# Sparse attention of 64 items: four buffers, memory keys and half of the memory values inside its loop, items looked ahead in another order

## The reference, cut to what matters

```python
y_conv = conformer_conv(conv_a, conv_b, w_dw, b_dw, ln_g, ln_b)   # depthwise conv of 31 taps, layer norm, SiLU
out = g[..., 0:1] * o_cmp + g[..., 1:2] * o_slc + g[..., 2:3] * o_win   # compressed, selected, window attention
h = h + jnp.concatenate([y_conv, y_nsa], axis=-1) @ w_out
h = h + memory_attention(rmsnorm(h, g1), rmsnorm(mem, g2), w_mem_q, w_mem_k, w_mem_v, w_mem_o)
h = h + peer(rmsnorm(h, g3), ...)   # 16 experts of 16384 for each of 8 heads and every token, gathered by rows
```

## Time and profile before

| | us |
|---|---|
| median of 3 runs | 2980.44 (2977.33 to 2980.55) |
| profiled execution | 2980.34, span 2978.5 |
| mean granted clock of TensorE | 0.907 |
| TensorE, VectorE, ScalarE, GpSimd busy in the span | 2604.3, 1440.5, 643.2, 596.9 |
| sparse attention loop (first score matmul to last value matmul) | about 1044 to 1286 |
| first matmul of the output product | 1325.84 |

### The profile page before, as it was taken

One profiled execution on the slowest core, in us unless ns is written; L12 is line 12 of the kernel. 1 busy time (PEld: TensorE's weight loads), 2 busy tenths in 40 slices (PEclk: granted clock), 3 DMA queues, 4 the chain that ended last, 5 costly groups with the idle time before them and its releaser, 6 DMA issues.

```text
span 2978.5 us, 22380 instructions
## 1 busy us (share of the span) xinstructions
PE 2604.3 (87%) x7486; PEld 1261.2 (42%) x7486; DVE 1440.5 (48%) x3647; ACT 643.2 (22%) x1514; POOL 596.9 (20%) x554
## 2 busy tenths in 40 slices
PE   6999999989979989999999899877778778778787
PEld 2456544435534545554454344333333333333232
DVE  0003113035342855322013666777777777777774
ACT  2000012116320132221122222222222122222221
POOL 0000000000000000000000243444444444344442
PEclk8999899999989975589999999999998998898988
DMA  8101042200111200012212899999999999999996
GB/s 350 56 29 57 28 184 85 85 0 1 43 49 60 85 15 0 1 57 85 85 43 95 322 380 378 420 421 421 421 422 421 421 421 420 419 418 416 417 412 264
DMA packets 83154, 648.49 MB, mean 218 GB/s; under 512 B 9329, under 2 KB 9617, under 8 KB 10978
## 3 DMA queue, kind: packets, MB, share of 16 engines
q0 software_dynamic: 75696, 551.95, 45.0%
q1 hardware_dynamic: 7346, 95.12, 8.4%
HBM read 644.93 MB, written 2.10 MB: 217 GB/s over the span
## 4 chain that ended last, share of the span: by engine, by line
PE 61%; DMA 23%; DVE 9%; ACT 2%; issue 2%; POOL 1%; ACTq 0%; DVEq 0%; POOLq 0%; SPq 0%; PEldq 0%
PE psum L506 23%; DMA arena<-in_peer_uv,newton 22%; PE psum L1057 12%; PE psum L1026 3%; PE psum L580 3%; PE psum L871 2%; PE psum L888 2%; DVE arena L1871 2%; PE psum L879 1%; PE psum L562 1%; PE psum L539 1%; PE psum L675 1%; PE psum L725 1%; PE psum L943 1%; ACT arena L1093 1%
## 5 line engine op out<-in xcount | busy, mean ns | idle before, releaser
L1057 PE MATMUL psum<-arena 128*128 128x512 f32 x2048 | 1006.9, 648 | 249.1 <-ACT arena L1371 248.7
L1057 PEld LDWEIGHTS psum<-arena 128*128 128x128 f32 x2048 | 415.3, 208 | 834.9 <-issue 834.8
L1871 DVE CUSTOM_DVE_ANT_0 arena<-arena 128x1024 f32<-128x1024 f32 x512 | 619.5, 1223 | 304.2 <-DMA arena<-in_peer_uv,newton 301.1
L2004 POOL DMA_INDIRECT arena<-in_peer_uv,newton x512 | 566.3, 1106 | 859.2 <-PE psum L1057 711.7
L506 PE MATMUL psum<-arena 128*128 128x512 f32 (+2 forms) x1824 | 698.2, 543 | 22.2 <-DVE arena L1543 8.0
L506 PEld LDWEIGHTS psum<-arena 128*128 128x128 f32 (+1 forms) x1824 | 346.3, 191 | 369.3 <-issue 347.9
L1093 ACT ACTIVATE arena<-psum 128x512 f32<-128x512 f32 (+8 forms) x335 | 177.5, 542 | 968.0 <-PE psum L506 398.1
L1371 ACT ACTIVATE arena<-ident,newton 128x128 f32<-128x128 f32 x512 | 166.5, 391 | 247.2 <-DVE newton L1880 240.2
L1362 ACT ACTIVATE arena<-arena 128x4 f32<-128x4 f32 (+1 forms) x148 | 30.2, 204 | 658.6 <-DVE arena L1871 658.5
L1026 PE MATMUL psum<-arena 128*128 128x512 f32 x256 | 119.3, 603 | 4.8 <-DVE arena L1543 4.5
L1599 DVE TENSOR_REDUCE small<-psum 128x1 f32<-128x768 f32 (+1 forms) x48 | 37.4, 780 | 123.4 <-PE psum L959 85.0
(11 more groups left out here) (257 smaller groups left out, 2022.4 us busy)
## 6 DMA issues: line engine op xcount, KB each, us to landing
arena<-in_weights SPq DMA_DIRECT2D x44, 2048.0 KB, 8.5
arena<-in_peer_uv,newton POOLq DMA_INDIRECT x512, 18.5
arena<-in_xin POOLq DMA_DIRECT2D x1, 3072.0 KB, 16.8
arena<-in_dft_l POOLq DMA_DIRECT2D x1, 2048.0 KB, 14.1
arena<-in_cmp_w POOLq DMA_DIRECT2D x1, 2048.0 KB, 7.5
out<-arena SPq DMA_DIRECT2D x4, 512.0 KB, 10.0
arena<-in_pool_band POOLq DMA_DIRECT2D x1, 1280.0 KB, 5.8
arena<-in_fnet_w POOLq DMA_DIRECT2D x1, 1024.0 KB, 20.8
```

The source lines that it names most:

```text
L1057: ins = mm(bank(j_y[t][q]), DIAG[i % 4], ROW[ROW_PLACE[i]][:, D + 512 * q:D + 512 * q + 512], start=(r == 0), stop=(r == 127))
L1871: v.tensor_tensor_reduce(out=u, in0=u, in1=HNT[:, i // 128, :], scale=1.0, scalar=0.0, op0=ALU.mult, op1=ALU.add, accum_out=DOTS[:, i:i + ...
L2004: g.indirect_dma_start(out=ROW[ROW_PLACE[i]][:, :], out_offset=None, in_=a["peer_uv"], in_offset=bass.IndirectOffsetOnAxis(ap=IDX[:, n, e: ...
```

## The change

`SM`, `P2` and `PT2` get four buffers each; other areas move to make room. The scores take banks 0 and 1 in turn instead of three, and bank 2 serves the memory keys, the sum of the conv output and the first half of the memory values, one job after the other.

TensorE's order for i becomes transposes of i, values of i-2, a memory step, scores of i+4 last; VectorE's is normalise i, masked maximum of i+3; ScalarE's is exponential of i+1, copy of i-1. A memory step is two 128x256 matmuls of the memory keys in items 10 to 33 and 38 to 45, and one 128x512 matmul of the memory values' first half in items 46 to 61. The memory norm moves to items 1 to 13, the conv taps to one in each of items 0 to 31, and the conv norm into items 34 to 49: sum at 34, centring at 35, squares at 37, second sum at 41, variance at 42, root at 43, inverse at 44, scaling at 46, SiLU at 49. The weights of the memory values are cut into two blocks: the first comes ahead of the output product's blocks, the second stays behind them. Behind the loop only the second half of the values is left.

```diff
-          ("mem_k", 2), ("out2", 2), ("mem_v", 2), ("mem_q", 2), ("mem_o", 2), ("peer_q", 4)]
+          ("mem_k", 2), ("mem_v_lo", 1), ("out2", 2), ("mem_v_hi", 1), ("mem_q", 2), ("mem_o", 2), ("peer_q", 4)]
...
-        SM = area(80, 2, L)
+        SM = area(88, 4, L)
...
-        P2 = area(72, 2, L)
-        PT2 = area(76, 2, L)
+        P2 = area(72, 4, L)
+        PT2 = area(80, 4, L)
...
-        SQ2 = area(72, 4, L)
+        SQ2 = area(144, 4, L)
...
-        MV = area(120, 2, D)
-        MQ = area(128, KC, L)
+        MV = area(136, 2, D)
+        MQ = area(96, KC, L)
...
-            if hh == 1:
+            if hh == 0:
                 j_rms_mem = [J.take(5)]
+            if hh == 5:
+                j_ln_cv_var = J.take(5)
             for m in range(8):
-                j_s2[8 * hh + m] = J.take((8 * hh + m) % 3)
+                j_s2[8 * hh + m] = J.take((8 * hh + m) % 2)
                 j_pt2[8 * hh + m] = J.take(3 + (8 * hh + m) % 2)
+        j_mk = [J.take(2) for _ in range(6)]
+        j_ln_cv = [[J.take(2)], [j_ln_cv_var]]
+        j_mk += [J.take(2) for _ in range(2)]
+        j_mv = [J.take(2) for _ in range(2)]
         J.align()
-        j_ln_cv = [J.turn(1)]
-        j_mk = J.turn(4)
-        j_ln_cv.append(J.turn(1))
-        j_mk += J.turn(4)
         j_rms_mq = J.turn(1)
         j_out2 = J.turn(8, [j_rms_mq[0][0]])
-        j_mv = J.turn(4)
+        j_mv += J.turn(2)
...
+            def memory_keys(c, first, last):
+                w = weights("mem_k", c // 4)
+                j = j_mk[c]
+                for k in range(first, last):
+                    if k == 0:
+                        claim(pe, j)
+                    pe.wait_ge(S["mem_ready"], k + 1)
+                    ins = mm(bank(j, LC), w[:, c % 4, k, :], MEMT[:, k, :], start=(k == 0), stop=(k == KC - 1))
+                if last == KC:
+                    done(ins, j)
+                    if c % 4 == 3:
+                        release_block(j)
+            def memory_values(b, t, first, last):
+                w = weights(("mem_v_lo", "mem_v_hi")[b], 0)
+                j = j_mv[2 * b + t]
...
+            def memory_step(i):
+                if 10 <= i < 34:
+                    n = i - 10
+                    memory_keys(n // 4, 2 * (n % 4), 2 * (n % 4) + 2)
+                elif 38 <= i < 46:
+                    n = i - 14
+                    memory_keys(n // 4, 2 * (n % 4), 2 * (n % 4) + 2)
+                elif 46 <= i < 62:
+                    n = i - 46
+                    memory_values(0, n // 8, n % 8, n % 8 + 1)
             cmp_scores(0)
-            for i in range(3):
+            for i in range(4):
                 scores2(i)
             for i in range(64):
-                if 1 <= i < 62:
-                    scores2(i + 2)
                 transpose2(i)
                 if i % 8 == 0:
                     cmp_transpose(i // 8)
-                    if i:
-                        values2(i - 1)
+                if i >= 2:
+                    values2(i - 2)
+                if i % 8 == 1:
                     cmp_values(i // 8)
-                else:
-                    values2(i - 1)
                 if i % 8 == 4 and i < 56:
                     cmp_scores(i // 8 + 1)
-                if i == 10:
+                if i == 2:
                     norm_sum(j_rms_mem[0], MEMSQ, 0, LC, KC, S["mem_sq"], 0)
+                if i == 34:
+                    norm_sum(j_ln_cv[0][0], CACC, 0, L, 4, S["conv_y"], 0)
+                if i == 41:
+                    norm_sum(j_ln_cv[1][0], SQ2, 0, L, 4, S["squared"], 32)
+                memory_step(i)
+                if i < 60:
+                    scores2(i + 4)
+            values2(62)
             values2(63)
-            norm_sum(j_ln_cv[0][0], CACC, 0, L, 4, S["conv_y"], 0)
-            pe.wait_ge(S["mem_ready"], KC)
-            for b in range(2):
-                w = weights("mem_k", b)
-                for c in range(4):
-                    feat(j_mk[4 * b + c], w[:, c, :, :], MEMT, 0, LC)
-                release_block(j_mk[4 * b + 3])
-                if b == 0:
-                    norm_sum(j_ln_cv[1][0], SQ2, 0, L, 4, S["squared"], 32)
...
-            for b in range(2):
-                w = weights("mem_v", b)
...
+            for t in range(2):
+                memory_values(1, t, 0, KC)
...
+            def exp2(i):
+                n = (ITEMS2[i][1] + 1) * P
+                if i >= 4:
+                    full(act, j_pt2[i - 4])
+                act.wait_ge(S["p_max"], N1 + i + 1)
+                fn(P2[:, i % 4, 0:n], SM[:, i % 4, 0:n], ACT.Exp, bias=nmx[:, i % 8:i % 8 + 1], scale=0.125,
+                   accum_out=rsum[:, i % 8:i % 8 + 1]).then_inc(S["p_exp"], 1)
+            def transposed2(i):
+                n = (ITEMS2[i][1] + 1) * P
+                if i >= 4:
+                    act.wait_ge(S["pt_used"], N1 + i - 3)
+                copy_out(j_pt2[i], PT2[:, i % 4, 0:n], n)
+            cmp_exp(0)
+            exp2(0)
             for i in range(65):
-                if i < 64:
-                    if i == 0:
-                        cmp_exp(0)
-                    n = (ITEMS2[i][1] + 1) * P
-                    after(i, j_pt2)
-                    act.wait_ge(S["p_max"], N1 + i + 1)
-                    fn(P2[:, i % 2, 0:n], SM[:, i % 2, 0:n], ACT.Exp, bias=nmx[:, i % 8:i % 8 + 1], scale=0.125,
-                       accum_out=rsum[:, i % 8:i % 8 + 1]).then_inc(S["p_exp"], 1)
+                if i + 1 < 64:
+                    exp2(i + 1)
                 if i >= 1:
-                    n = (ITEMS2[i - 1][1] + 1) * P
-                    if i >= 3:
-                        act.wait_ge(S["pt_used"], N1 + i - 2)
-                    copy_out(j_pt2[i - 1], PT2[:, (i - 1) % 2, 0:n], n)
+                    transposed2(i - 1)
                     if (i - 1) % 8 == 0:
                         cmp_pt((i - 1) // 8)
-                    if i % 8 == 6 and i < 56:
-                        cmp_exp(i // 8 + 1)
...
-            squares(SQ2, CACC, 0, L, 4, S["centered"], 24)
-            for c in range(4):
-                copy_out(j_mk[c], MK[:, c, :], LC)
-            root(j_ln_cv[1][0], RS2[:, :], L)
-            for c in range(4, 8):
-                copy_out(j_mk[c], MK[:, c, :], LC)
-            for c in range(4):
-                act.wait_ge(S["scaled"], 24 + c + 1)
-                fn(CACC[:, c, :], CACC[:, c, :], ACT.Silu, bias=vc("conv_ln_b", c), scale=vc("conv_ln_g", c))\
-                    .then_inc(S["mix_conv"], 1)
+                if i % 8 == 6 and i < 56:
+                    cmp_exp(i // 8 + 1)
+                if i == 1:
+                    act.wait_ge(S["mem_loaded"], 16)
+                    for k in range(KC):
+                        fn(MEMSQ[:, k, :], MEMT[:, k, :], ACT.Square).then_inc(S["mem_sq"], 1)
+                if i == 4:
+                    root(j_rms_mem[0], RSM[:, :], LC)
+                if i in (14, 18, 22, 26, 30, 34):
+                    copy_out(j_mk[i // 4 - 3], MK[:, i // 4 - 3, :], LC)
+                if i == 37:
+                    squares(SQ2, CACC, 0, L, 4, S["centered"], 24)
+                if i in (42, 46):
+                    copy_out(j_mk[i // 4 - 4], MK[:, i // 4 - 4, :], LC)
+                if i == 43:
+                    root(j_ln_cv[1][0], RS2[:, :], L)
+                if i in (54, 62):
+                    copy_out(j_mv[(i - 54) // 8], MV[:, (i - 54) // 8, 0:512])
+                if i == 49:
+                    for c in range(4):
+                        act.wait_ge(S["scaled"], 24 + c + 1)
+                        fn(CACC[:, c, :], CACC[:, c, :], ACT.Silu, bias=vc("conv_ln_b", c), scale=vc("conv_ln_g", c))\
+                            .then_inc(S["mix_conv"], 1)
...
-            for b in range(2):
-                for t in range(2):
-                    copy_out(j_mv[2 * b + t], MV[:, t, 512 * b:512 * b + 512])
+            for t in range(2):
+                copy_out(j_mv[2 + t], MV[:, t, 512:D])
...
             masked_max(1)
+            masked_max(2)
             for i in range(64):
...
-                normalise(N1 + i, None, P2[:, i % 2, 0:(qt + 1) * P], gates_tok[:, qt, 3 * head + 1 + br:3 * head + 2 + br])
-                if i + 2 < 64:
-                    masked_max(i + 2)
+                normalise(N1 + i, None, P2[:, i % 4, 0:(qt + 1) * P], gates_tok[:, qt, 3 * head + 1 + br:3 * head + 2 + br])
+                if i + 3 < 64:
+                    masked_max(i + 3)
                 if i % 8 == 5 and i < 56:
                     cmp_shift(hh + 1)
-                if i % 4 < 3:
+                if i < 32:
                     conv_taps(1)
-                if i == 11:
+                if i == 3:
                     variance(j_rms_mem[0], D, LC)
-                if i == 14:
+                if i == 5:
                     inverse(RSM[:, :], LC)
-                if 16 <= i < 16 + KC:
-                    k = i - 16
+                if 6 <= i < 6 + KC:
```

(38 more changed lines are left out.)

17 lines of the change are left out of this document (2 added, 15 removed).

## The result

| | before | after |
|---|---|---|
| median of all runs, us | 2979.29 (2977.33 to 2980.55, 4 runs) | 2932.84 (2931.25 to 2933.26, 4 runs) |
| ratio | 1 | 0.9844, 95% interval 0.9827 to 0.9861 |
| profiled execution, us | 2980.34 (span 2978.5) | 2933.26 (span 2931.4) |
| first transposes of the loop, us from the start | 1049.1 | 1051.0 |
| first matmul of the output product | 1325.84 | 1296.09 |

What follows compares the result with a forecast made beforehand. TensorE in program order at 1.2 GHz was taken to bound the attention loop. Savings of 38.2 us up to the output product, then 2.6 and 14.0, made 54.8 off 2980.34: 2925.5 us, range 2905 to 2960.

Steps and rivals of the forecast that it cites:

- (a): Behind the loop: norm sums, memory keys and SiLU wait go, 0.9 us stays; output product starts at full clock, 2.6 us saved.
- (b): Memory values behind the output product: half move into the loop, 14.0 us saved; the other half still covers VectorE's norm.
- (c): Loop matmul work at 2.4 GHz: 1.03 us a memory step, periods 26.1 us with memory, 17.9 without; 202 us altogether.
- (d): Lookahead in the loop: ScalarE's copy and exponential leave the chain; TensorE leads, 3.3 us an item against VectorE's 1.9 to 2.6.
- the engines' chain sets the pace: Rival for the loop: four buffers don't shorten 3.45 us items, memory work only fills holes; 2944 us, counted in main case.
- (e): VectorE blocks in the loop stall TensorE: 4.5 us at item 5's inverse, 2.5 at 35, 3.3 at 44; 14 together.
- (f): Lower clock remaining in the loop: 6 us at start, 8 for items 6 to 11, 3 after 35, 2.5 after 44; 19.5.
- (g): Loop's start and end: first transposes 1.1 us later, at 1050.2; last copies cost 1 and the attention copy 0.9.
- The slower one: Rival: clock stays at 1.2 GHz where memory work runs in the loop, 2.66 us more per item; 3055 us, chance 8%.
- The clock comes back late: Rival: after VectorE's blocks the loop stays at 0.50 for a period each, 16 memory items; 2964 us, chance 14%.
- The stalls are too short to lose the clock: Rival: the loop keeps its clock through VectorE's blocks, 13.5 us of (f) and 4 of (e) drop out; 2908 us, chance 15%.

Runs made afterwards that it cites:

- e3: The changed kernel with memory keys, conv norm and all values put back behind the loop, four buffers and lookahead kept: 2938.36 us.
- e8: e7 plus memory steps without a gap in items 8 to 55 and the conv norm's centring, inverse and scaling in pieces: 2902.60 us.
- e10: The changed kernel with unread filler matmuls, four records of 128x256 on 64 rows, in each of items 3 to 9: 2919.93 us.
- e7: The changed kernel with memory keys from item 8, the memory norm's inverse split over items 4 and 5, no conv taps in items 4 to 6: 2914.94 us.
- e6: The changed kernel with memory keys two items earlier, from item 8, and their scalings two at a time in items 6 to 9: 2923.59 us.
- e2: The kernel before with two score banks and four unread records of 128x256 on 64 rows added in each item: 2964.96 us.
- e1: The kernel before with two score banks and four unread records of 128x256 on 128 rows added in each item: 2965.92 us.
- e9: The changed kernel with unread filler matmuls, four records of 128x256 on 128 rows, in each of items 3 to 9: 2922.84 us.

## Why the prediction was right, and where it was off

The forecast was 2925.5 with a range of 2905 to 2960, and 2932.84 lies in it, on the slow side. By the prediction's steps:

(a) held. The wait that is left ahead of the output product is 0.94 us against 0.9, and its clock is at 1.00 from the first matmul: from there to the memory values before took 1391.12 - 1325.84 = 65.28 us, after 1358.73 - 1296.09 = 62.64. That is 2.64 less, against 2.6.

(b) held. One block of values is gone, and the other covers the query norm, which ends at 1365.96 + 5.39 = 1371.35, with 1.3 us to spare (the values end at 1358.73 + 13.90 = 1372.63). From the output product on the sum gave -16.6, and the spans give -17.4.

(c) held. At the upper clock a period with memory was forecast at 26.1 us; the three full ones took 26.6, 26.4 and 26.1. The estimate of 17.9 us for one without memory was a little low: e3's last three average 19.5, one of them with a short low stretch. A memory step costs (26.4 - 19.5) / 8 = 0.86 us, or 0.96 with the two heads that saw no low clock, and not 1.03; the two errors cancel.

(d) held as to who waits. The scores are what the masked maximum waits for, 106.9 us in 54 waits, and TensorE doesn't wait for every transpose. The rival that the engines' chain sets the pace falls: with nothing to fill its holes, e3's items take 2.3 to 2.6 us at 1.00, not the 3.45 of before.

(e) held: 4.53 us at item 6 against 4.5, and 13.2 in all against 14. At items 36 and 45 the waits are 3.05 and 3.60 us, against 2.5 and 3.3.

(f) is the term that was mis-sized. It had 8 us, between 0 and 13, for items 6 to 11 at the lower clock. The clock stayed down from item 6 through item 13 and into 14, 41 us, with the memory steps of items 10 to 13 in it. From the transposes of item 6 to those of item 16 (1076.5 to 1122.6) it took 46.1 us; at the upper clock it is about 30: 26.4 less two memory steps of 0.94 (between the 0.86 and 0.96 above) for items 8 to 15, and an estimated 5.5 for items 6 and 7. So the term is 16 us, and the 8 missing make the miss; the other stretches cancel (items 32 to 47 took 3.3 us more than forecast, items 0 to 5 and the stretch from item 56 on 3.1 less, and the 2.8 for small waits covers what the rest took more). The step behind it was that dense 128-row work "has always brought 1.00": items 10 to 13 have it and stayed at 0.50 with the start of 14 for 22 us (1094.3 to 1116.8), while items of the same make stayed at 1.00 from 1117 on. The rows that the step rested on the earlier trace rows showed only blocks of 128-row matmuls with nothing between them, never a mixture. After the centring at 35, 14 us at 0.50 cost more than the 3 forecast (the period took 33.6 against 31.2: 26.1, less four memory steps, and 3.7, 2.5 and 3 for the norm sum, the stall and the clock), and the head behind it, 37.4, was right within 1.

(g) held within 0.8 us: first transposes at 1051.0 against 1050.2.

**The rivals.** The slower one (the clock stays down where memory work runs) needed 21 items more at 1.2 GHz than counted. There were a few more, which is its mechanism in small, and after's own clock from 1117 on shows that it doesn't go on. "The clock comes back late" was right for one of the stalls and gave the sign of the miss. "The stalls are too short to lose the clock", 2908, was wrong of after, where the clock fell at waits of 4.53, 3.05 and 3.60 us. e8, in which the stalls are cut, came to 2902.60, but it lost the clock at item 6 with a wait of 1.77 us, so that the length of a stall doesn't settle it alone.

**Right for a reason too narrow.** The prediction gave nearly the whole gain in the loop to the memory work on 128 rows and the lookahead only an item's worth of slack. e3 took the memory work away and kept 42 of the 47 us; by the prediction's reasoning it should have come to 2973 to 2985. That the clock would come back was right; that it needed the 128-row work was not. The sum uses only that the clock is up, whatever brings it, and so it came out although the cause was too narrow: that part is luck. With e10, where 64-row filler did as well, what the runs leave is this: once down, the clock stayed down for long in this loop, and more matmul work in its items, of either kind, ended that sooner; so did, by less, a shorter stall (1085.2 in e7 against 1090.7 in e6). How the chip weighs 64-row against 128-row work stays open, and so does what makes the clock fall.

## What to carry to other kernels

When a busy TensorE shows a clock of 0.50, ask first what brings the level back, and count a stage at both levels: here heads with the same matmuls cost 31.8 or 18.3 us (e3). After a planned stall put matmul work into the very next items (e6: 9 us), and cut the stall itself into pieces: e8 did both and won 30 us from after, almost only by changing the order of the same work. Don't count on a short stall to hold the clock; look at the granted clock behind it. Two edits that both let the clock come back don't add; price them together, and undo each alone to see it.

## What the runs showed of the hardware

- The granted clock has a memory of its level: items with the same matmuls ran at 0.50 for 22 us in after (items 10 to 13 and the start of 14) and at 1.00 for 75 us right behind (1117 to 1192), TensorE recorded busy for nearly all of both.
- A fall needs no long wait: the clock fell at 1074.9 in e8 with a wait of 1.77 us, and at 1181.2 in e2 with none longer than 0.7 us; in e1 it stayed at 1.00 through one of 1.97 us (at 1113.8).
- More work can take less time: four records more in each item (e1) took 14 us off the kernel before, and in seven items (e9) 10 us off after.
- Matmuls on 64 rows run side by side with matmuls on the other 64. In e2 an item took 1.79 us where filler and scores use different halves, and 2.44 where they use the same one; e1's filler on 128 rows gave 2.64 for the same item (1226.66 to 1229.30). e10 has it too, by its timeline:

```profile
1086.49 0.71 PE L931 MATMUL psum<-arena 64*128 64x256 f32 x1
1086.50 0.81 PE L874 MATMUL psum<-arena 64*128 64x384 f32 x1
```

The Trainium skill ("TensorE: Matmul & The Clock Gate", "The mechanism" under the packing of small matmuls) says that matmuls on tiles of the array that don't conflict overlap. The traces agree; I had not expected it of two streams that nobody had arranged for it.
